# Recurrent gate products of 64 channels on the four quarters of the matmul array, second gate's tanh in two half-height pieces

## Chip, cores and metric

The kernel runs on one core of a Trainium2 chip. The time is the device time of one execution in microseconds (us). A core has a matmul engine (PE), a vector engine (DVE), an activation engine (ACT), GpSimd (POOL) and a sync engine (SP) that here only issues the loads of weights. Each has its own instruction stream, and they meet at semaphores.

## What is computed

One program computes two transformer-like layers, one after the other, for 512 tokens of width 1024. The change touches a small part of the first: the gates of a recurrent unit. There are 1024 channels in 16 blocks of 64, and each block has its own 64x64 weights for two gates:

```python
def rg_lru(x, wa, ba, wx, bx, lam):
    r = jax.nn.sigmoid(block_diag_linear(x, wa, ba).astype(jnp.float32))
    i = jax.nn.sigmoid(block_diag_linear(x, wx, bx).astype(jnp.float32))
    log_a = -LRU_C * r * jax.nn.softplus(-lam.astype(jnp.float32))
    a = jnp.exp(log_a)
    mult = jnp.sqrt(-jnp.expm1(2.0 * log_a))
    u = mult * (i * x.astype(jnp.float32))
    # then h[t] = a[t] * h[t-1] + u[t] along the tokens

# around it, for each token:
xc = causal_depthwise_conv(rnn_x, conv_w, conv_b)
y_rnn = rg_lru(xc, ...) * jax.nn.gelu(rnn_gate)
```

Before it, one projection (`h @ w_in`) gives all inputs of the layer, the recurrent ones among them; after it come sparse attention, the output projections and a feed-forward part, and then the second layer.

## The kernel before

Activations lie transposed: channels on the 128 partitions, the 512 tokens along the free dimension. Every large product is cut into "jobs" of 128 output channels. A job (`job`, `block_of`, lines 325 to 327) runs 24 matmuls of 128x512: for each of 8 slices of the contraction the products high*high, high*low and low*high of operands that were split into two parts. The weights of a job come by DMA (SP); ACT makes the high part (`split`, line 907), POOL subtracts it to get the low part in four pieces (line 296), and PE waits for `lo_ready`. Four weight slots are in flight. DVE takes each finished job out of PSUM (`take`, line 1450) and counts `job_taken`; a job waits until the one two before it was taken.

The jobs have one fixed order. The change lies in the recurrence, whose order is written out by hand in a loop of four turns (`for i in range(4)`, in each engine's stream). Each turn handles channel tiles f = 2i and 2i+1 of 128 channels (two blocks of 64 each):

- PE: job k+2, job k+3, `rnn_gates(2i)`, job k+4, `rnn_gates(2i+1)`, job k+5, with k = 15 + 4i. `rnn_gates` (line 433) waits for `conv_done` and issues two f32 matmuls of 128x512, one for each gate. Their weights `rgw` are a 128x128 matrix with two 64x64 blocks on the diagonal and zeros elsewhere. Each f32 matmul shows as two records.
- ACT: `gelu_square`, two `split`s, `conv_head(f+1)` (line 1009), `gelu_square`, then `rnn_decay(f)`, `gelu_tanh`, a `split`, `rnn_decay(f+1)`, `gelu_tanh`, a `split`, `conv_head(f+2)`, two square roots (`rnn_root`, line 1035) and two `rnn_high` (line 1039). `rnn_decay` (lines 1026 to 1031) is two tanh out of PSUM, a wait for their end, two exp and a third tanh.
- DVE: `take` of jobs k+2 and k+3, `conv_tail(f+1)`, two `gelu_inner`, `take` of k+4, `rnn_input(f)` and `rnn_input(f+1)` (each waits for `rnn_a`, the last instruction of `rnn_decay`), `take` of k+5, `conv_tail(f+2)`, `rnn_scan(f)` and `rnn_scan(f+1)` (wait for `rnn_root`; the scan is line 1593), and `rnn_low` of both, which wait for `rnn_high`.

In the fourth turn DVE has the maxima of the attention scores (line 1607) between `rnn_input(6)` and `rnn_input(7)`, and PE runs the first scores (line 440) after `rnn_gates(7)`. Then `pair(0)` begins: PE runs a job, turns the values (line 450) and waits for `rlo_ready` of 8, the low part of the recurrence's last tile, before the first job that multiplies the recurrence's output `b_hi`, `b_lo`. ACT's order in that place is `rnn_high(6)`, six exponentials (line 1073), a `split`, `rnn_high(7)`.

The two gates of a tile go to two PSUM banks: tiles alternate between `(s_ps[0], s_ps[1])` and `(s_ps[2], o_ps)`.

Of the kernel before, what the change touches and what calls it, by code (L numbers as in the profile page):

```python
# [29 lines left out]
ACT = mybir.ActivationFunctionType  # L30
# [3 lines left out]
P = 128  # L34
# [82 lines left out]
def build(nc, w_all, x_t, mem_t, vecs, consts, rg_w, consts2, row_table, out):  # L117
    with ExitStack() as ctx:
# [3 lines left out]
        def sem(name):  # L122
            return ctx.enter_context(nc.semaphore(name))
# [28 lines left out]
        def tiles(i, n=1):  # L152
            return arena[:, i:i + n, :]

        def flat(ap):
            return ap.rearrange("p a b -> p (a b)")
# [23 lines left out]
        rc = [arena[:, 2, :], arena[:, 3, :]]  # L180
        rr = [arena[:, 4, :], arena[:, 5, :]]
        ri = [arena[:, 6, :], arena[:, 7, :]]
        ra = [arena[:, 17, :], arena[:, 18, :]]
        rt = [arena[:, 8, :], arena[:, 19, :]]
        rgw = flat(tiles(24, 4)).rearrange("p (f c) -> p f c", c=2 * P)
# [44 lines left out]
        rnn_ps = ((s_ps[0], s_ps[1]), (s_ps[2], o_ps))  # L230
# [21 lines left out]
        def s(name):  # L252
            if name not in SEMS:
                SEMS[name] = sem(name)
            return SEMS[name]
# [59 lines left out]
        def _(pe):  # L315
            mm, tp = nc.tensor.matmul, nc.tensor.transpose

            def block_of(k, kts, hi, lo, n=T, last=7, pieces=False):

                sl, ps = k % SLOTS, bank(k)  # L320
                for kt in kts:
                    if pieces and kt % (KT // PIECES) == 0:
                        pe.wait_ge(s("lo_ready"), k * PIECES + kt * PIECES // KT + 1)
                    c = slice(kt * P, kt * P + P)
                    mm(ps[:, 0:n], w_hi[:, sl, c], hi[:, kt, 0:n], start=kt == 0, stop=False)  # L325
                    mm(ps[:, 0:n], w_hi[:, sl, c], lo[:, kt, 0:n], start=False, stop=False)  # L326
                    ins = mm(ps[:, 0:n], w_lo[:, sl, c], hi[:, kt, 0:n], start=False, stop=kt == last)  # L327
                return ins
# [59 lines left out]
            for t in range(QT):  # L388
                ins = tp(t_ps[1][:, t * P:t * P + P], p1[:, 0, t * P:t * P + P], ident)
# [22 lines left out]
            for k in range(8):  # L412
# [8 lines left out]
                for t in range(QT):  # L421
                    ins = mm(sums[:, t, 2 * k:2 * k + 2], sq[:, (k + 1) % 2, t * P:t * P + P], halves,
                             start=True, stop=True)
# [4 lines left out]
            def rnn_gates(f):  # L428

                u = f % 2  # L430
                pe.wait_ge(s("conv_done"), f + 1)
                for c in range(2):
                    ins = mm(rnn_ps[u][c][:], rgw[:, f, c * P:c * P + P], rc[u], start=True, stop=True)
                ins.then_inc(s("rnn_mm"), 1)

            def scores(p, which):
# [70 lines left out]
            for i in range(4):  # L507
                k = J_RNN + 4 * i
                job(k + 2, a_hi, a_lo)
                job(k + 3, a_hi, a_lo)  # L510
                rnn_gates(2 * i)
                job(k + 4, a_hi, a_lo)
                rnn_gates(2 * i + 1)
                if i == 3:
                    pe.wait_ge(s("k_normed"), 2)
                    pe.wait_ge(s("rnn_tanh"), 7)
                    scores(0, ATT_FIRST)
                job(k + 5, a_hi, a_lo)
# [42 lines left out]
            for c in range(2):  # L561
                ins = mm(s_ps[c][:], w_alpha[:, c * P:c * P + P], in2[:, 12, :], start=True, stop=True)
# [4 lines left out]
            for h in range(4):  # L567
# [4 lines left out]
                for t in range(QT):  # L572
                    ins = tp(t_ps[h % 2][:, t * P:t * P + P], in2[:, 4 + h, t * P:t * P + P], ident)
# [5 lines left out]
            for c in range(2):  # L579
                for t in range(QT):  # L580
                    ins = tp(t_ps[c][:, t * P:t * P + P], in2[:, 2 + c, t * P:t * P + P], ident)
# [17 lines left out]
            for m in range(4):  # L599
# [3 lines left out]
                for h in range(4):  # L603
                    out_r = slice(64 * (h % 2), 64 * (h % 2) + 64)
                    for n in (2 * m, 2 * m + 1)[0:1 if m == 3 else 2]:
                        r = slice(64 * (n % 2), 64 * (n % 2) + 64)
                        ins = mm(t_ps[n % 2][out_r, h * P:h * P + P], g_ke[r, m, h * 64:h * 64 + 64],
                                 g_vt[h][r, m, :], start=True, stop=True)
# [20 lines left out]
            for c2 in range(2):  # L629
# [7 lines left out]
                for half in range(2):  # L637
                    h = 2 * c2 + half
                    for t in range(QT):
                        c = slice(t * P, t * P + P)  # L640
                        mm((o_ps, s_ps[1])[half][:, c], g_vt[h][:, t, :], g_at[h][:, c], start=t == 0, stop=False,
                           skip_group_check=True)
                for n in range(1, 8):
                    for half in range(2):
                        r = slice(64 * half, 64 * half + 64)
                        c = slice(64 * n, 64 * n + 64)
                        ins = mm((o_ps, s_ps[1])[half][:, c], g_st[r, c2, n, :], g_qd[r, c2, c],
                                 start=False, stop=n == 7, skip_group_check=True)
# [9 lines left out]
            for t in range(QT):  # L658
                ins = tp(t_ps[0][:, t * P:t * P + P], in2[:, 18, t * P:t * P + P], ident)
# [200 lines left out]
            for gi, g in enumerate(FF2_GROUPS):  # L860
# [17 lines left out]
                for kt in (g - 2, g - 1):  # L878
                    pe.wait_ge(s("hlo_ready"), done - g + kt + 1)
                    ins = block_of(k, [kt], a_hi, a_lo, last=g - 1)  # L880
# [6 lines left out]
            for t in range(QT):  # L887
# [3 lines left out]
                ins = mm(sums[:, t, 20:22], sq[:, 1, t * P:t * P + P], ones2, start=False, stop=True)  # L891
# [6 lines left out]
        def _(act):  # L898
            fn = nc.scalar.activation
# [50 lines left out]
            for f in range(8):  # L950
# [16 lines left out]
               scale=float((64 ** -0.5) * (8 ** -0.5))).then_inc(s("iw_ready"), 1)  # L967
# [32 lines left out]
            def scol(c0, f):  # L1000
                return small[:, c0 + f:c0 + f + 1] if isinstance(f, int) else small[:, ds(f + c0, 1)]
# [18 lines left out]
            def rnn_decay(f):  # L1020

                u = f % 2
                act.wait_ge(s("rnn_mm"), f + 1)
                if f >= 2:
                    act.wait_ge(s("rlo_ready"), f - 1)
                fn(rr[u], rnn_ps[u][0][:], ACT.Tanh, scale=0.5, bias=scol(32, f)).then_inc(s("act_step"), 1)
                fn(ri[u], rnn_ps[u][1][:], ACT.Tanh, scale=0.5, bias=scol(40, f)).then_inc(s("rnn_tanh"), 1)
                act.wait_ge(s("rnn_tanh"), f + 1)
                fn(ra[u], rr[u], ACT.Exp, scale=scol(16, f), bias=scol(16, f)).then_inc(s("act_step"), 1)
                fn(rt[u], rr[u], ACT.Exp, scale=scol(8, f), bias=scol(8, f)).then_inc(s("act_step"), 1)  # L1030
                fn(rr[u], rr[u], ACT.Tanh, scale=scol(24, f), bias=scol(24, f)).then_inc(s("rnn_a"), 1)
# [10 lines left out]
            for i in range(4):  # L1042
                k, f = J_RNN + 4 * i, 2 * i
                gelu_square(f)
                split(k + 5)
                conv_head(f + 1)
                split(k + 6)
                gelu_square(f + 1)
                rnn_decay(f)
                gelu_tanh(f)  # L1050
                split(k + 7)
                rnn_decay(f + 1)
                gelu_tanh(f + 1)
                split(k + 8)
                if i < 3:
                    conv_head(f + 2)
                rnn_root(f)
                rnn_root(f + 1)
                if i < 3:
                    rnn_high(f)  # L1060
                    rnn_high(f + 1)
# [45 lines left out]
            with act.Fori(0, 2) as i:  # L1107
                for c in range(4):
# [4 lines left out]
                       bias=scol(56, i * 4 + c)).then_inc(s("sg_ready"), 1)  # L1113
# [1065 lines left out]
```

## Time and profile before

| | before |
|---|---|
| median of 3 runs | 1635.64 us (1634.28 to 1636.27) |
| the profiled execution | 1634.13 us, of it span 1632.3 us |
| PE busy | 1597.4 us (98%) |
| DVE busy | 722.0 us (44%) |
| ACT busy | 671.3 us (41%) |
| POOL busy | 797.6 us (49%) |

All times in the rows are counted from the span's start. A row of the timeline has start, length, engine, line, operation, output<-input, shape and count, and in brackets the idle time before it and who ended it. Matmul records overlap, so it is their starts that tell the pace. PEld are the weight loads. A row of the windows has, for a stretch, the busy time of PE, PEld, DVE, ACT and POOL, then the granted PE clock (1.00 is full), the share of the DMA engines and the rate.

### The profile page before, as it was taken

The numbers are of one execution on the slowest core, as the hardware profiler recorded it, in microseconds if no ns is written. First come the engines' busy times: TensorE is split into PE (matmuls) and PEld (weight loads), VectorE is DVE, ScalarE is ACT, GpSimd is POOL, SyncE is SP. The second block draws the span as 40 slices with busy tenths as digits, with TensorE's granted clock in tenths as the row PEclk, the third lists the DMA queues.
The fourth block names the chain that finished last, engine by engine and source line by source line (L and its number), as shares of the span: only waits on it lengthen the run. The fifth ranks groups of instructions, "written<-read, shape, count | busy, mean of one in ns | idle before, by whom it ended". The sixth has DMA issues, their size and how long they took to land. (4 is left out here: it accounts for less than half of the span.)

```text
span 1632.3 us, 22641 instructions
## 1 busy us (share of the span) xinstructions
PE 1597.4 (98%) x7646; PEld 1294.2 (79%) x7646; DVE 722.0 (44%) x1373; ACT 671.3 (41%) x1082; POOL 797.6 (49%) x1060
## 2 busy tenths in 40 slices
PE   7999998999999999999999999999999999999997
PEld 6787776777888888888888877678978888888886
DVE  5597996664233212121132442744223552452354
ACT  5415675544424423232233424643544442342332
POOL 5244573323454555555555541246635555565453
PEclk9999999999999999999999999999999999999999
DMA  5222221112323232323233222132422223223231
GB/s 185 87 84 78 72 92 64 52 65 104 103 90 103 91 103 90 103 90 103 90 101 103 90 79 65 41 113 94 129 77 91 91 90 116 90 90 104 90 103 65
DMA packets 45061, 149.77 MB, mean 92 GB/s; under 512 B 4600, under 2 KB 7808, under 8 KB 44992
## 3 DMA queue, kind: packets, MB, share of 16 engines
q1 hardware_dynamic: 38592, 139.48, 26.2%
q10 hardware_dynamic: 6400, 9.36, 1.7%
q8 instruction: 45, 0.74, 0.2%
q14 instruction: 24, 0.20, 0.0%
HBM read 146.58 MB, written 2.11 MB: 91 GB/s over the span
## 5 line engine op out<-in xcount | busy, mean ns | idle before, releaser
L296 POOL TENSOR_TENSOR w_lo<-w_raw,w_hi 128x256 fp32r<-128x256 f32 x1056 | 797.4, 787 | 810.6 <-ACT w_hi L907 809.8
L325 PE MATMUL job<-a_hi,w_hi 128*128 128x512 f32 (+1 forms) x1056 | 406.4, 385 | 10.0 <-POOL w_lo L296 9.8
L327 PE MATMUL job<-a_hi,w_lo 128*128 128x512 f32 (+1 forms) x1056 | 398.2, 377 | 0.0
L326 PE MATMUL job<-a_lo,w_hi 128*128 128x512 f32 (+1 forms) x1056 | 398.0, 377 | 0.0
L907 ACT ACTIVATE w_hi<-w_raw 128x1024 fp32r<-128x1024 f32 x264 | 275.1, 1050 | 281.2 <-PE job L327 271.5
L325 PE MATMUL job<-b_hi,w_hi 128*128 128x512 f32 x952 | 375.6, 395 | 5.1 <-DVE b_lo L1450 4.8
L327 PE MATMUL job<-b_hi,w_lo 128*128 128x512 f32 x952 | 371.3, 390 | 0.0
L326 PE MATMUL job<-b_lo,w_hi 128*128 128x512 f32 x952 | 371.0, 390 | 0.0
L325 PEld LDWEIGHTS job<-a_hi,w_hi 128*128 128x128 f32 x1056 | 199.0, 188 | 52.6 <-DVE a_lo L1447 11.0
L326 PEld LDWEIGHTS job<-a_lo,w_hi 128*128 128x128 f32 x1056 | 199.2, 189 | 37.2 <-issue 1.9
L327 PEld LDWEIGHTS job<-a_hi,w_lo 128*128 128x128 f32 x1056 | 199.0, 188 | 37.1
L325 PEld LDWEIGHTS job<-b_hi,w_hi 128*128 128x128 f32 x952 | 179.2, 188 | 42.5 <-DVE b_lo L1450 5.1
L327 PEld LDWEIGHTS job<-b_hi,w_lo 128*128 128x128 f32 x952 | 179.0, 188 | 37.8
L326 PEld LDWEIGHTS job<-b_lo,w_hi 128*128 128x128 f32 x952 | 179.2, 188 | 36.1 <-issue 0.2
L1450 DVE TENSOR_TENSOR arena<-arena,job 128x512 f32<-128x512 f32 (+1 forms) x92 | 62.9, 686 | 263.3 <-PE job L327 249.9
L1450 DVE TENSOR_TENSOR arena<-job,rstd 128x512 f32<-128x512 f32 (+1 forms) x117 | 80.0, 687 | 167.0 <-PE job L327 141.6
L1447 DVE SCALAR_TENSOR_TENSOR arena<-arena,vec 128x512 f32<-128x512 f32 x112 | 103.7, 926 | 60.4 <-ACT arena L1398 53.0
L922 ACT ACTIVATE sq<-arena 128x512 f32<-128x512 f32 x48 | 30.1, 630 | 114.8 <-DVE arena L1450 111.6
L1398 ACT ACTIVATE arena<-arena,vec 128x512 f32<-128x512 f32 x44 | 35.6, 809 | 87.8 <-DVE arena L1450 87.8
L1450 DVE TENSOR_TENSOR a_lo<-arena,a_hi 128x512 f32 (+1 forms) x58 | 40.0, 692 | 64.0 <-ACT a_hi L1129 42.2
L1128 ACT ACTIVATE arena<-arena 128x512 f32<-128x512 f32 x32 | 20.2, 632 | 106.5 <-DVE arena L1447 106.5
L1447 DVE SCALAR_TENSOR_TENSOR arena<-job,rstd 128x512 f32<-128x512 f32 x32 | 22.1, 691 | 91.2 <-PE job L327 86.6
(259 smaller groups left out, 1368.0 us busy)
## 6 DMA issues: line engine op xcount, KB each, us to landing
w_raw<-w_all SPq DMA_DIRECT2D x264, 512.0 KB, 3.4
arena<-x_t ACTq DMA_DIRECT2D x8, 512.0 KB, 6.9
arena<-rg_w ACTq DMA_DIRECT2D x1, 1024.0 KB, 7.8
arena<-row_table ACTq DMA_DIRECT2D x1, 1024.0 KB, 6.1
arena<-mem_t ACTq DMA_DIRECT2D x1, 1024.0 KB, 6.7
out_t<-arena SPq DMA_DIRECT2D x4, 256.0 KB, 2.2
out_t<-arena ACTq DMA_DIRECT2D x4, 256.0 KB, 2.2
arena<-consts ACTq DMA_DIRECT2D x1, 384.0 KB, 3.8
```

The costliest lines, as they stand in the source:

```text
L296: nc.gpsimd.tensor_tensor(w_lo[:, sl, c], raw[:, sl, c], w_hi[:, sl, c].bitcast(F32), ALU.subtract).then_inc(s("lo_ready"), 1)
L325: mm(ps[:, 0:n], w_hi[:, sl, c], hi[:, kt, 0:n], start=kt == 0, stop=False)
L326: mm(ps[:, 0:n], w_hi[:, sl, c], lo[:, kt, 0:n], start=False, stop=False)
L327: ins = mm(ps[:, 0:n], w_lo[:, sl, c], hi[:, kt, 0:n], start=False, stop=kt == last)
L907: fn(w_hi[:, sl], raw[:, sl], ACT.Copy).then_inc(s("hi_ready"), 1)
L922: fn(sq[:, f % 2, :], src, ACT.Square).then_inc(s("sq_ready"), 1)
L1128: fn(act_s[:, c % 2, :], act_t[:, c % 2, :], ACT.Square).then_inc(s("ff_sq"), 1)
L1398: fn(f_c[u], f_u[u][:, PAD:PAD + T], ACT.Identity, scale=vcol("conv_w2", col + 88), bias=vcol("conv_b2", col)).then_inc(s("f_head"), 1)
L1447: return v.scalar_tensor_tensor(out=out_, in0=a, scalar=sc, in1=b, op0=op0, op1=op1)
L1450: return v.tensor_tensor(out_, a, b, op)
```

## The change

`rnn_gates` issues four matmuls of 64 contraction rows and 64 output channels instead of two of 128 and 128; the zero blocks are no longer multiplied. The first gate's halves go to the same partitions as before. The second gate's halves are written to the other half of the partitions of their bank, so that the four products stand on four different quarters of the array. ACT puts them back: the second tanh becomes two instructions of 64 partitions and 512 columns, each reading one half of the bank and writing the other half of `ri`.

```diff
                 u = f % 2
                 pe.wait_ge(s("conv_done"), f + 1)
-                for c in range(2):
-                    ins = mm(rnn_ps[u][c][:], rgw[:, f, c * P:c * P + P], rc[u], start=True, stop=True)
+                for half in range(2):
+                    r, other = slice(64 * half, 64 * half + 64), slice(64 - 64 * half, P - 64 * half)
+                    mm(rnn_ps[u][0][r], rgw[r, f, 64 * half:64 * half + 64], rc[u][r], start=True, stop=True)
+                    ins = mm(rnn_ps[u][1][other], rgw[r, f, P + 64 * half:P + 64 * half + 64], rc[u][r],
+                             start=True, stop=True)
                 ins.then_inc(s("rnn_mm"), 1)
...
                 fn(rr[u], rnn_ps[u][0][:], ACT.Tanh, scale=0.5, bias=scol(32, f)).then_inc(s("act_step"), 1)
-                fn(ri[u], rnn_ps[u][1][:], ACT.Tanh, scale=0.5, bias=scol(40, f)).then_inc(s("rnn_tanh"), 1)
+                even, odd = slice(0, 64), slice(64, 128)
+                fn(ri[u][even], rnn_ps[u][1][odd], ACT.Tanh, scale=0.5, bias=scol(40, f)[even]).then_inc(s("act_step"), 1)
+                fn(ri[u][odd], rnn_ps[u][1][even], ACT.Tanh, scale=0.5, bias=scol(40, f)[odd]).then_inc(s("rnn_tanh"), 1)
                 act.wait_ge(s("rnn_tanh"), f + 1)
```

## Rows read from the trace of the kernel before

**Rows 1.** Windows of 10 us around the end of the recurrence.
```profile
235.00:245.00 10.00, 10.00 (x50) 7.63 (x47) 9.83 (x19) 7.36 (x10) 8.64 (x10) 1.00 0.38 114
245.00:255.00 10.00, 5.08 (x23) 3.53 (x21) 7.31 (x15) 8.00 (x21) 6.91 (x7) 0.85 0.26 96
```

**Rows 2.** Waits of PE from 100 to 262 us: total, times, longest.
```profile
PE job L325 <- DVE b_lo L1450: 4.8, 1, 4.8
```

**Rows 3.** Timeline of the gate products: weight loads of one set, starts of two sets.
```profile
149.11 0.19 PEld L433 LDWEIGHTS score<-arena 128*128 128x128 f32 x1 [0.24 <-issue]
149.54 0.19 PEld L433 LDWEIGHTS score<-arena 128*128 128x128 f32 x1 [0.24 <-issue]
...
173.97 1.88 PE L433 MATMUL score<-arena 128*128 128x512 f32 x4
...
224.56 1.88 PE L433 MATMUL score<-arena 128*128 128x512 f32 x4
```

**Rows 4.** Timeline of ACT over the third turn of the recurrence.
```profile
198.03 0.63 ACT L1039 ACTIVATE b_hi<-arena 128x512 fp32r<-128x512 f32 x1 [1.95 <-DVE arena L1447]
...
203.62 0.69 ACT L1026 ACTIVATE arena<-score,small 128x512 f32<-128x512 f32 x1
204.21 0.68 ACT L1027 ACTIVATE arena<-score,small 128x512 f32<-128x512 f32 x1
...
211.23 0.80 ACT L1031 ACTIVATE arena<-arena,small 128x512 f32<-128x512 f32 x1
...
223.46 0.63 ACT L1039 ACTIVATE b_hi<-arena 128x512 fp32r<-128x512 f32 x1 [1.96 <-DVE arena L1447]
```

**Rows 5.** Timeline of DVE over the same turn.
```profile
199.31 1.28 DVE L1450 TENSOR_TENSOR arena<-job,rstd 128x512 f32<-128x512 f32 x2
...
212.06 1.45 DVE L1447 SCALAR_TENSOR_TENSOR arena<-arena 128x512 f32<-128x512 f32 x2 [1.70 <-ACT arena L1031]
...
222.74 0.69 DVE L1447 SCALAR_TENSOR_TENSOR arena<-sq,arena 128x512 f32<-128x512 f32 x1
```

**Rows 6.** Timeline of ACT in the first turn and at the recurrence's end.
```profile
157.80 0.69 ACT L1026 ACTIVATE arena<-score,small 128x512 f32<-128x512 f32 x1 [1.26 <-PE o L433]
...
231.78 0.80 ACT L1031 ACTIVATE arena<-arena,small 128x512 f32<-128x512 f32 x1
...
240.24 1.15 ACT L1035 ACTIVATE arena<-arena 128x512 f32<-128x512 f32 x2
...
245.48 0.64 ACT L1039 ACTIVATE b_hi<-arena 128x512 fp32r<-128x512 f32 x1 [3.06 <-DVE arena L1447]
...
251.77 0.61 ACT L1039 ACTIVATE b_hi<-arena 128x512 fp32r<-128x512 f32 x1
```

**Rows 7.** Timeline of DVE at the recurrence's end.
```profile
232.14 0.68 DVE L1450 TENSOR_TENSOR arena<-job,rstd 128x512 f32<-128x512 f32 x1
...
238.57 1.83 DVE L1447 SCALAR_TENSOR_TENSOR arena<-arena 128x512 f32<-128x512 f32 x2
...
252.42 0.80 DVE L1450 TENSOR_TENSOR b_lo<-arena,b_hi 128x512 fp32r<-128x512 f32 x1 [2.42 <-ACT b_hi L1039]
```

**Rows 8.** Timeline of PE where the first job on the recurrence's output starts.
```profile
253.27 0.80 PE L325 MATMUL job<-b_hi,w_hi 128*128 128x512 f32 x1 [4.84 <-DVE b_lo L1450]
```

**Rows 9.** Timeline of PE in the second layer: 64x64 products, eight matmuls a row.
```profile
957.03 0.67 PE L607 MATMUL turn<-arena 64*64 64x128 f32 x16
963.30 0.67 PE L607 MATMUL turn<-arena 64*64 64x128 f32 x16
```

**Rows 10.** Timeline of PE in the second layer: a restart after idle time.
```profile
1023.24 0.71 PE L699 MATMUL turn<-cst,arena 128*128 128x128 f32 x3 [2.83 <-DVE arena L1454]
```

**Rows 11.** Windows behind the restarts of rows 8 and rows 10.
```profile
253.00:259.00 6.00, 4.67 (x15) 3.62 (x16) 5.58 (x22) 3.97 (x9) 2.42 (x3) 0.51 0.30 89
...
1024.00:1026.00 2.00, 2.00 (x6) 1.52 (x6) 1.93 (x8) 0.47 (x1) 0.50 (x1) 0.50 0.25 37
```

**Rows 12.** Groups of DVE by form: one operation on 64 partitions.
```profile
L1447 DVE SCALAR_TENSOR_TENSOR arena<-arena,vec,turn 64x512 f32<-64x512 f32 x1 | 0.7, 739 | 2.8 <-PE turn L366 2.8
```

## The prediction, as it was put on record

> **What bounds the kernel now.** I read the page first: PE is busy for 98% of the span, so the first guess is that every microsecond taken from PE is one gained. The question is whether that holds where the change is. The windows around the end of the recurrence show that it does not quite: from 235 to 245 us PE is busy throughout, and in the next 10 us it is busy for only 5.08, with a granted clock of 0.85 [rows 1]. The list of PE's waits names the cause: one wait of 4.8 us, for the low part of the recurrence's output [rows 2], which ends when PE restarts at 253.27 us [rows 8]. So the end of this stage is not set by PE. It is set by a chain through ACT and DVE, and the timelines of these two tell what that chain is made of.
>
> I followed it through the third turn of the loop. ACT's `rnn_high` at 198.03 us waits for DVE. From there ACT runs without a gap until its L1031 of the second tile, 211.23 + 0.80 = 212.03 us [rows 4]. DVE has been idle for 1.70 us by then and starts `rnn_input` on it at 212.06. From there DVE runs without a gap to the product that starts at 222.74 and ends at 223.43 us [rows 5], and ACT's next `rnn_high` starts at 223.46 [rows 4]. That is a closed ring of ACT and DVE with no PE in it, and one turn of it takes 223.46 - 198.03 = 25.43 us. PE's own turn is (224.56 - 173.97) / 2 = 25.30 us [rows 3]. PE is therefore level with the ring but no longer ahead of it. Only the first turn is different: there ACT waits 1.26 us for the gate products before it can start the tanh at 157.80 us [rows 6].
>
> **The change part by part.**
>
> *PE, removed and added.* The weight loads of a set are 0.43 us apart (149.54 - 149.11) [rows 3], there are four of them, so a set costs PE 1.72 us, and eight sets 13.8 us. The nearest rows to what replaces them are the 64x64 products of the second layer: eight matmuls of 128 columns, that is 16 records, take 0.67 us from first start to last end [rows 9]. A 128x512 record takes 0.43 us, so 16 records of 128 columns one after another would need 16 x 0.43 / 4 = 1.72 us; only if four quarters work at once do they fit. The path cost of that group is its repeat, 963.30 - 957.03 = 6.27 us, less the one job in it; four jobs and two gate sets make a turn of 25.30, so a job is (25.30 - 3.44) / 4 = 5.47 us, and the group costs 0.80 us against 0.43 of pure streaming. I charge the same 0.37 us on top of 2 x 0.43 for a new set: 1.23 us, a saving of about 0.5 us a set, 4 us in all, on PE. The bounds are 0.86 us a set (no charge) and 4 x 0.86 = 3.44 us (no overlap at all).
>
> The quarters of the new set differ from those rows in one thing: both halves of the rows write the same PSUM bank at the same time, on different partitions. Should that make them take turns, a set costs 1.72 us as before.
> The Trainium skill speaks on this against the change: the page "TensorEngine Tiling (Array Packing)", section "Restrictions and Gotchas", says that different row tiles cannot access the same PSUM bank simultaneously, by which a set would stay at 1.72 us; no row here shows two row halves in one bank.
>
> *ACT, added.* One more instruction in each `rnn_decay`. The step from the first tanh to the second is 204.21 - 203.62 = 0.59 us [rows 4]. The new pieces have half the partitions but all 512 columns. No ACT row has 64 partitions; a DVE operation on 64x512 took 0.739 us [rows 12], no less than its kin on 128 partitions (0.69 us in rows 5). So I take the full 0.59 us for each extra piece; the bounds are 0.3 (half, were it to go by partitions) and 0.7. Each turn has two of them, and both lie in ACT's part of the ring: +1.18 us a turn. What is queued behind the new instruction on ACT: the two exp, L1031, the gelu tanh, the `split` and all of the second `rnn_decay`. DVE waits for L1031, POOL for the `split` and PE through POOL; a job's low part is ready over 4 us before PE needs it, so the `split`s cost nothing as long as this margin is not used up.
>
> *The sum, on the path that sets the end.*
> - Turn 0: ACT no longer waits for PE. Its queue before the second tanh ends 1.26 us before 157.80, now 0.59 later: 157.13 us; PE's products are there by then (two sets faster by 0.5 each). So the second tile starts 0.67 earlier and has 0.59 more to do: -0.1 us. If PE stays at 1.72 a set, this is +0.6 instead.
> - Turns 1 and 2: the ring turns twice, from ACT's `rnn_high` of turn 0 to that of turn 2: 2 x 1.18 = +2.4 us. DVE's wait of 1.70 us for L1031 only moves: inside the turn the first L1031 comes 0.59 later and pushes DVE by some 0.4, which this wait takes in.
> - Turn 3: the second L1031 no longer decides, as DVE has the attention maxima before `rnn_input(7)`, which starts at 238.57 us [rows 7]. What counts is the first: L1031 ends at 231.78 + 0.80 = 232.58 us [rows 6], now 0.59 later, 233.17; DVE is through with its `take` at about 232.7 [rows 7]. DVE is pushed by 0.45 us. The square root at 240.24 us [rows 6] moves by 1.18 and comes just in time for the scan. From there the chain of `rnn_high(6)` at 245.48, the exponentials, `rnn_high(7)` at 251.77 [rows 6] and the low part at 252.42 us [rows 7] moves as one: +0.45 us.
> - Sum: -0.1 + 2.4 + 0.45 = +2.7 us for PE's restart at 253.27 us. After it PE is full again and all that follows moves along.
>
> PE's saving goes into its waits. In turns 1 to 3 job k+4 may not start before DVE has taken job k+2, at 199.31 + about 0.7 in the old timing [rows 5]; as the ring moves later and PE earlier, PE will stand still there for some 0.3 us in turn 1 and 2.5 us in turns 2 and 3, and the wait of 4.84 us [rows 8] grows to 6 or 7. Idle time has a price of its own: behind 2.83 us of it [rows 10] the granted clock was 0.50, the 1.2 GHz level, in a window of 2 us, and behind the wait of 4.84 us it was 0.51 over 6 us [rows 11]. A stretch of 2 to 6 us at the half level in turn 2 or 3 makes job k+4 end 1 to 3 us later; DVE's `take` of it and the next gate set have 1 to 2 us of room for that, so I count 0 here, with 0 to 1.4 us as bounds.
>
> The profiled execution took 1634.13 us; with 2.7 more it is 1636.8. It lies 1.5 us below the median of the runs shown, so against the median the forecast is 1635.64 + 2.7 = 1638.3 us.
>
> **The rivals.**
> 1. *The extra instructions lie on the ring (forecast).* 1638.3 us, by itself 1637.4 to 1639.5.
> 2. *The halves of one bank take turns.* PE gains nothing, ACT still pays: turn 0 gives +0.6 instead of -0.1, so 1639.0 us. PE's turn of 25.30 is still shorter than the ring's 26.6, so it costs no more than this. For it: no row has this pattern. Against it: the halves are on different partitions.
> 3. *Idle time brings the low clock into the loop.* Forecast or rival 2 plus up to 1.4 us, or a fall in more than one turn: 1639.5 to 1641.5 us. For it: the stop of 2.5 us is near the 2.83 us after which the clock was low. Against it: the next step that needs PE has 1 to 2 us of room.
> 4. *PE is the bound after all, and the change is faster.* If ACT's pieces cost 0.3 us each or if the ring had slack that I did not see, the ring would turn at PE's pace, and PE's 0.5 us a set would come through in the first three turns, 3 us, with the last turn still held by the tail: 1632.5 to 1635 us. It decides from the point where ACT's extra time per turn is below PE's saving and there is slack of over 1 us in the ring. Against it: ACT shows no gap between 198.03 and 212.03, DVE none from there to 223.43.
> 5. *The quarters do not overlap.* Then PE's turn is 25.30 + 2 x 1.72 = 28.7 us, PE is the bound, and the seven intervals to `rnn_gates(7)` plus that set cost about 8 x 1.72 = 13.8 us: about 1649 us. Rows 9 speak against it.
>
> **How the numbers follow.** The chances: forecast 0.54, rival 2 0.17, rival 3 0.19, rival 4 0.08, rival 5 0.02. The range reaches over the first three and the upper part of rival 4: 1635.5 to 1641.0 us. What a measurement of this kernel can tell from no change is about 0.2%, 3.3 us: 1632.4 to 1638.9. The forecast lies inside this, near its edge; of its own 0.54 I give 0.38 to "same" and 0.15 to "slower"; of rival 2 about half each; rival 3 is slower but for a small part; rival 4 is mostly "same". Together: faster 0.03, same 0.57, slower 0.40.
>
> **What would show it.** In the changed trace: a gate set with eight records whose starts lie within about 0.9 us and the next job about 1.2 us after the first; two tanh pieces of the second gate, of 0.68 us, 0.59 apart; ACT's `rnn_high` of turns 1 and 2 26.6 us apart instead of 25.43; new PE waits for DVE's `take` of about 2.5 us in turns 2 and 3; PE's restart on the recurrence's output at about 256 us after a wait of 6 to 7. Wrong would be: pieces of clearly less than 0.6 us, a ring that still turns in 25.4 us, a restart before 253.3 us, or a time that comes from anywhere behind the restart, where nothing of the change lies.

## The result, and the profile after

The changed kernel takes 1640.48 us (median of 11 runs, 1638.55 to 1640.80) against 1636.0 us for the kernel before in the same sessions (11 runs, 1634.28 to 1636.39): 4.5 us more, a ratio of 1.0026 with a 95% interval of 1.0018 to 1.0034. The forecast was 1638.3 us with a range of 1635.5 to 1641.0.

The page of the changed kernel, part 1: PE has as much work as before and a longer span.

```profile
span 1638.9 us, 22713 instructions
...
PE 1597.7 (97%) x7678; PEld 1293.1 (79%) x7678; DVE 716.6 (44%) x1373; ACT 677.6 (41%) x1090; POOL 793.9 (48%) x1060
```

The two profiled spans differ by 6.6 us, the medians by 4.5: the executions of either kernel fall into two groups about 1.7 us apart, and the profile of before is one of the lower group, that of after one of the upper. Part of the difference lies in the last 13 us, in code that the change does not touch: PE is busy there for 2.88 us at a clock of 0.66 before, and for 4.23 us at 0.53 after. The windows of the last 13 us, before first and after second:

```profile
1620.00:1633.00 13.00, 2.88 (x22) 2.61 (x22) 5.58 (x10) 2.18 (x3) 0.00 (x0) 0.66 0.43 162
```
```profile
1626.00:1639.00 13.00, 4.23 (x22) 3.84 (x22) 5.54 (x9) 1.35 (x2) 0.00 (x0) 0.53 0.43 162
```

So I compare the stretch in which the change acts: from ACT's first `conv_head` (145.76 us before, 146.17 after; the 0.41 is from the start of the program) to PE's restart on the recurrence's output. Before it ends at 253.27 us [rows 8], after at 257.98: 107.51 against 111.81 us, 4.30 more. That is nearly the whole of the 4.5.

**PE.** The timeline of PE in the changed kernel, one gate set and its neighbours:

```profile
209.36 0.39 PE L327 MATMUL job<-a_hi,w_lo 128*128 128x512 f32 x1
209.68 0.64 PE L434 MATMUL score<-arena 64*64 64x512 f32 x1
209.68 0.64 PE L435 MATMUL o<-arena 64*64 64x512 f32 x1
209.69 0.64 PE L434 MATMUL score<-arena 64*64 64x512 f32 x1
209.70 0.64 PE L435 MATMUL o<-arena 64*64 64x512 f32 x1
210.16 0.59 PE L434 MATMUL score<-arena 64*64 64x512 f32 x1
210.16 0.59 PE L435 MATMUL o<-arena 64*64 64x512 f32 x1
...
210.69 0.50 PE L325 MATMUL job<-a_hi,w_hi 128*128 128x512 f32 x1
211.03 0.39 PE L326 MATMUL job<-a_lo,w_hi 128*128 128x512 f32 x1
```

All four quarters start within 0.02 us, although the two of each gate write halves of one bank. From the record before the set to the second one of the next job it is 211.03 - 209.36 = 1.67 us; less two ordinary steps of 0.227, the set costs 1.22 us. The same two records around a set in the kernel before:

```profile
173.75 0.39 PE L327 MATMUL job<-a_hi,w_lo 128*128 128x512 f32 x1
...
175.92 0.40 PE L326 MATMUL job<-a_lo,w_hi 128*128 128x512 f32 x1
```

They are 2.17 us apart, less the same two steps 1.72 us, as [rows 3] say.

**Where PE's gain went.** PE's waits from 100 to 270 us in the changed kernel (before: only that of rows 2 is longer than 2 us):

```profile
PE job L325 <- DVE b_lo L1455: 6.5, 1, 6.5
PE job L325 <- DVE arena L1455: 4.6, 3, 2.7
PE turn L470 <- ACT acc L1071: 1.1, 1, 1.1
PE turn L453 <- DVE arena L1455: 0.4, 1, 0.4
```

The wait at the end has grown from 4.8 to 6.5 us, and there are three new ones (0.89, 2.65 and 1.02 us, one in each of the turns 1 to 3) for DVE's `take`. Behind the one of 2.65 us the clock was low for a while: PE's restart, and the windows around it, with 0.93 and 0.76 in the column of the clock.

```profile
202.40 0.47 PE L325 MATMUL job<-a_hi,w_hi 128*128 128x512 f32 x1 [2.65 <-DVE arena L1455]
```
```profile
200.00:204.00 4.00, 1.60 (x6) 1.36 (x7) 3.62 (x6) 3.70 (x6) 1.53 (x3) 0.93 0.00 0
204.00:210.00 6.00, 6.00 (x24) 4.45 (x26) 5.11 (x6) 5.88 (x9) 6.00 (x6) 0.76 0.29 87
```

**The ring.** ACT over the third turn, the lines that answer to [rows 4]:

```profile
200.30 0.63 ACT L1044 ACTIVATE b_hi<-arena 128x512 fp32r<-128x512 f32 x1 [1.96 <-DVE arena L1452]
...
205.89 0.69 ACT L1029 ACTIVATE arena<-score,small 128x512 f32<-128x512 f32 x1
206.60 0.69 ACT L1031 ACTIVATE arena<-score,small 64x512 f32<-64x512 f32 x1
207.31 0.68 ACT L1032 ACTIVATE arena<-score,small 64x512 f32<-64x512 f32 x1
208.03 0.81 ACT L1034 ACTIVATE arena<-arena,small 128x512 f32<-128x512 f32 x1
...
215.18 0.80 ACT L1036 ACTIVATE arena<-arena,small 128x512 f32<-128x512 f32 x1
...
227.26 0.63 ACT L1044 ACTIVATE b_hi<-arena 128x512 fp32r<-128x512 f32 x1 [1.95 <-DVE arena L1452]
```

A turn takes 227.26 - 200.30 = 26.96 us instead of 25.43 [rows 4], and ACT's part of it, from `rnn_high` to the end of the second L1036, 15.68 instead of 14.00: 0.84 for each of the two tanh groups. A piece of 64 partitions takes 0.69 us, as long as a full one; but the steps are 0.71 and 0.71 us, where the step between the two full tanh was 0.59. DVE's part is shorter by 0.16: its first two products after the second L1036 take 1.29 us together instead of 1.45 [rows 5], as POOL's burst now ends before they start. The 4.30 us of the stretch split as follows: turn 0, from the first `conv_head` to its second `rnn_high` at 173.32, +0.30; turns 1 and 2, 53.94 instead of 50.85, +3.09; turn 3 and the tail +0.91.

### The profile page after: what moved, and what is told of

Read it like the earlier page. It is cut to its first block and busy times, and to the rows that moved or that the text cites. A ratio compares the mean times of both kernels' runs of the same rounds, so it can differ in the third digit from the quotient of the medians.

```text
span 1638.9 us, 22713 instructions
## 1 busy us (share of the span) xinstructions
PE 1597.7 (97%) x7678; PEld 1293.1 (79%) x7678; DVE 716.6 (44%) x1373; ACT 677.6 (41%) x1090; POOL 793.9 (48%) x1060
```

## The experiments

Each kernel was timed beside the kernel before, in four sessions whose medians of before were 1636.00, 1635.96, 1636.04 and 1635.75 us; each ratio is taken inside its session. The stretch is that from the first `conv_head` to PE's restart, in the profiled execution; the last column is its difference to before.

| run | ratio to before (95%) | median us | stretch us | stretch against before |
|---|---|---|---|---|
| before | | 1636.0 | 107.51 | |
| the change | 1.0026 (1.0018 to 1.0034) | 1640.48 | 111.81 | +4.30 |
| quarters only | 0.9993 (0.9984 to 1.0002) | 1634.77 | 106.41 | -1.10 |
| halves only | 1.0029 (1.0018 to 1.0040) | 1640.65 | 111.75 | +4.24 |
| extra full tanh | 1.0016 (1.0007 to 1.0025) | 1638.27 | 110.47 | +2.96 |
| change, split moved | 1.0045 (1.0031 to 1.0058) | 1642.46 | 114.81 | +7.30 |
| change, early product | 1.0025 (1.0016 to 1.0034) | 1639.48 | 110.84 | +3.33 |
| before, early product | 0.9996 (0.9987 to 1.0005) | 1635.71 | 107.21 | -0.30 |
| before, `rnn_high(7)` early | 0.9987 (0.9978 to 0.9996) | 1633.19 | 105.04 | -2.47 |
| before, both | 0.9984 (0.9975 to 0.9993) | 1632.72 | 104.81 | -2.70 |
| both and copies early | 0.9969 (0.9958 to 0.9980) | 1630.20 | 104.79 | -2.72 |
| the same with the change | 0.9994 (0.9985 to 1.0003) | 1634.19 | 108.43 | +0.92 |
| the same with quarters only | 0.9962 (0.9948 to 0.9976) | 1629.42 | 103.51 | -4.00 |

**1. The quarters alone.** The changed kernel with the old second tanh, so that the second gate's halves stay swapped (it leaves out putting them back):

```diff
-                even, odd = slice(0, 64), slice(64, 128)
-                fn(ri[u][even], rnn_ps[u][1][odd], ...)
-                fn(ri[u][odd], rnn_ps[u][1][even], ...)
+                fn(ri[u], rnn_ps[u][1][:], ACT.Tanh, scale=0.5, bias=scol(40, f)).then_inc(s("rnn_tanh"), 1)
```

> Only the products change: four 64x64 quarters, and one full-height tanh of 128x512 for the second gate, so the two halves of that gate stay swapped (the part left out is the swap). Theory A (a ring of ACT and DVE sets the recurrence, PE does not): the ring keeps its 25.4 us a turn, only the first turn gains because ACT no longer waits 1.26 us for PE; PE's restart on the recurrence's output comes 0.7 to 1.0 us earlier than before, about 1635.2 us, ratio 0.9995. Theory B (PE is the bound and its saving of 0.5 us a set comes through): ring at PE's pace, 24.4 us a turn, restart 3 to 4 us earlier, about 1632.5 us, ratio 0.998.

1634.77 us, 1.2 less than before, of which the interval cannot tell the sign for certain; the stretch is 1.10 us shorter. The ring turns at its old pace, from 197.84 to 223.21 us in ACT's timeline, 25.37 us:

```profile
197.84 0.63 ACT L1042 ACTIVATE b_hi<-arena 128x512 fp32r<-128x512 f32 x1 [1.95 <-DVE arena L1450]
...
223.21 0.63 ACT L1042 ACTIVATE b_hi<-arena 128x512 fp32r<-128x512 f32 x1 [1.96 <-DVE arena L1450]
```

Eight sets at 0.5 us each would be 4 us; 1.1 arrive. The rest is in PE's waits: 6.2 us before the restart and 1.7 for `take`. That is theory A.

**2. The halves alone.** The kernel before with the second tanh in two straight pieces, each of which reads and writes the same half of the partitions (a crossed piece reads one half and writes the other):

```diff
-                fn(ri[u], rnn_ps[u][1][:], ACT.Tanh, scale=0.5, bias=scol(40, f)).then_inc(s("rnn_tanh"), 1)
+                even, odd = slice(0, 64), slice(64, 128)
+                fn(ri[u][even], rnn_ps[u][1][even], ACT.Tanh, scale=0.5, bias=scol(40, f)[even]).then_inc(s("act_step"), 1)
+                fn(ri[u][odd], rnn_ps[u][1][odd], ACT.Tanh, scale=0.5, bias=scol(40, f)[odd]).then_inc(s("rnn_tanh"), 1)
```

> Only the tanh changes: the old two 128x128 products, and the second tanh in two pieces of 64 partitions, each straight (no piece crosses to the other half). Theory A (the extra piece on the ring is the whole loss, and a piece of half height keeps the step from overlapping, 0.71 us instead of 0.59): rnn_decay 0.84 us longer, ring 26.9 to 27.0 us a turn, the first turn loses 0.85 more because it still waits for PE; restart about 4.8 us later than before, about 1641 us, ratio 1.003. Theory C (it is the crossing of halves that makes the steps 0.71 us, not the height): steps 0.59, rnn_decay 0.59 us longer, ring 26.4, restart about 3.3 us later, about 1639.3 us, ratio 1.002. Theory D (the loss comes from PE's new stops and the low clock, not from ACT): about the time before, ratio 1.000.

1640.65 us: without any quarter on PE the loss is as large. PE's stops for `take` sum up to 2.4 us here, and none has the low clock behind it (1.00 in both windows from 200 to 210 us), so theory D falls. That the total equals the changed kernel's is a coincidence of two differences. Its 4.24 us are 0.68 in turn 0, 2.80 in turns 1 and 2 and 0.76 behind them, where the changed kernel has 0.30, 3.09 and 0.91: turn 0 still waits for the old products, and each group is cheaper. ACT's timeline gives the steps:

```profile
205.72 0.69 ACT L1026 ACTIVATE arena<-score,small 128x512 f32<-128x512 f32 x1
206.31 0.67 ACT L1028 ACTIVATE arena<-score,small 64x512 f32<-64x512 f32 x1
207.01 0.69 ACT L1029 ACTIVATE arena<-score,small 64x512 f32<-64x512 f32 x1
207.73 0.82 ACT L1031 ACTIVATE arena<-arena,small 128x512 f32<-128x512 f32 x1
```

Neither of my two readings of the step holds as written. From the full tanh to the even half the step is 0.59, from the even to the odd half 0.70. So it is not the height, and it is not only the crossing.

**3. One more full tanh.** The kernel before with

```diff
+                fn(rt[u], rnn_ps[u][1][:], ACT.Tanh, scale=0.5, bias=scol(40, f)).then_inc(s("act_step"), 1)
                 fn(ri[u], rnn_ps[u][1][:], ACT.Tanh, scale=0.5, bias=scol(40, f)).then_inc(s("rnn_tanh"), 1)
```

> The old products and the old second tanh, with one extra full-height tanh of 128x512 of the same PSUM bank ahead of it, written to a tile that is free then. It measures what one more ACT instruction costs with all three at full height. If the height is what makes the steps 0.71 us: steps 0.59, rnn_decay 0.59 us longer, ring 26.4 us, about 1639.3 us, ratio 1.002. If any third tanh costs 0.85 us: the same as the halves-only run, ring 27.0 us, about 1641 us.

```profile
205.10 0.69 ACT L1026 ACTIVATE arena<-score,small 128x512 f32<-128x512 f32 x1
205.69 0.68 ACT L1027 ACTIVATE arena<-score,small 128x512 f32<-128x512 f32 x1
206.26 0.69 ACT L1028 ACTIVATE arena<-score,small 128x512 f32<-128x512 f32 x1
206.98 0.81 ACT L1030 ACTIVATE arena<-arena,small 128x512 f32<-128x512 f32 x1
```

Steps of 0.59 and 0.57 us: one more instruction of full height costs the 0.58 that I had put into the forecast, and the ring turns in 26.43 us (199.51 to 225.94). The time is 1638.27, what the forecast had for the changed kernel, 1638.3. With the runs 2 and 3 and the changed kernel beside each other, the steps are 0.56 to 0.59 us where source and target start at the same partition as those of the instruction ahead, and 0.68 to 0.72 us in every step where they do not. The cleanest pair is full to straight (0.59) against full to crossed (0.71): height, target and bias are the same, and only the source starts at partition 64 instead of 0. In the other long steps source and target change together, and one piece of 64 partitions follows another, so a change of the target alone, and two half pieces with the same start, stay untested. The changed kernel has two long steps in each group (full to crossed, crossed to crossed), the straight halves have one, the full tanh none: `rnn_decay` is longer by 0.84, 0.72 and 0.58 us.

**4. A split moved on ACT.** The changed kernel with

```diff
                 rnn_decay(f)
                 gelu_tanh(f)
-                split(k + 7)
                 rnn_decay(f + 1)
+                split(k + 7)
                 gelu_tanh(f + 1)
```

> The changed kernel with one weight split (0.95 us of ACT) moved from between the two rnn_decay of a turn to behind the second. It touches nothing on PE or in the gates. Theory A (ring): ACT's part of the ring is 0.95 us shorter, of which the gelu tanh takes back some 0.2; ring about 26.2 us a turn instead of 26.97; the square roots of the last turn keep their place behind the same instructions, so restart 1.5 to 2.3 us earlier than in the changed kernel, about 1638.5 us, ratio to before 1.0015. Theory D (PE's stops are the cause, ACT is not the bound): no change against the changed kernel, 1640.5 us, ratio 1.0027.

1642.46 us: 2 us slower than the changed kernel, where I had expected 2 us faster; a miss. A turn takes 230.12 - 202.09 = 28.03 us. ACT's part is shorter as expected (202.09 to 216.98, 14.89 instead of 15.68 us), but DVE's part, from the start on L1036 to the end of its last product, has grown from 11.21 to 13.07 us. In the timelines of DVE and POOL:

```profile
223.52 1.22 DVE L1455 TENSOR_TENSOR arena<-arena 128x512 f32<-128x512 f32 x1
224.78 1.64 DVE L1598 TENSOR_TENSOR_SCAN arena<-arena 128x512 f32<-128x512 f32 x1
226.45 1.04 DVE L1452 SCALAR_TENSOR_TENSOR arena<-sq,arena 128x512 f32<-128x512 f32 x1
```
```profile
218.00 8.94 POOL L296 TENSOR_TENSOR w_lo<-w_raw,w_hi 128x256 fp32r<-128x256 f32 x8 [5.89 <-ACT w_hi L910]
```

and in the changed kernel:

```profile
217.53 3.97 POOL L296 TENSOR_TENSOR w_lo<-w_raw,w_hi 128x256 fp32r<-128x256 f32 x4 [2.49 <-ACT w_hi L910]
```
```profile
221.97 0.68 DVE L1455 TENSOR_TENSOR arena<-arena 128x512 f32<-128x512 f32 x1
222.69 1.23 DVE L1598 TENSOR_TENSOR_SCAN arena<-arena 128x512 f32<-128x512 f32 x1
```

The two splits now lie side by side, POOL works on both in one burst of 8.9 us, and under it the same DVE operations take 1.22 instead of 0.68 and 1.64 instead of 1.23 us. DVE also waits 0.17 us for the gelu tanh, which now comes behind a split. The time still follows the ring; what failed was my claim that the move touches nothing else on it. That the operations take longer while POOL works is what these durations show; what the two engines contend for was not tested.

**5 and 6. The product that does not need all of `rnn_decay`.** In DVE's `rnn_input`, in the changed kernel (5) and in the kernel before (6):

```diff
-                dve.wait_ge(s("rnn_a"), f + 1)
+                dve.wait_ge(s("rnn_tanh"), f + 1)
                 dve.wait_ge(s("conv_done"), f + 1)
                 did(stt(ri[u], ri[u], 1.0, rc[u], ALU.add, ALU.mult))
+                dve.wait_ge(s("rnn_a"), f + 1)
                 stt(rt[u], rt[u], 1.0, rr[u], ALU.add, ALU.mult).then_inc(s("rnn_m"), 1)
```

> The changed kernel; DVE's first product of rnn_input (the one that uses the second gate) waits for the two tanh pieces instead of the last instruction of rnn_decay, so 0.61 us of DVE leave the ring and nothing on ACT, PE or POOL changes. Theory A (ring of ACT and DVE): ring 26.97 - 0.6 = 26.4 us a turn, three turns of it: PE's restart 1.8 us earlier than in the changed kernel, stretch from the first conv_head to the restart 110.0 us against 111.8; about 1638.7 us, ratio to before 1.0017. Theory D (PE's stops are the cause): no change, 1640.5 us.

> The kernel before with the same move. Theory A: the ring could turn in 24.8 us, but PE's turn is 25.3, so PE becomes the bound of turns 1 and 2: 25.3 us a turn, restart 0.4 to 1.0 us earlier than before, about 1635.2 us, ratio 0.9995. If the ring had been bound by PE already: no change, 1636.0 us.

5: 1639.48 us, a ratio of 1.0025 that cannot be told from the changed kernel's 1.0026. The stretch can: it is 0.97 us shorter with PE untouched, and the ring takes 26.72 us, 0.25 less and not the 0.6 that I expected, so half of the expected gain came. The timeline of DVE shows who is next, `conv_head` on ACT:

```profile
217.61 3.62 DVE L1452 SCALAR_TENSOR_TENSOR arena<-arena,vec 128x512 f32<-128x512 f32 x3 [0.16 <-ACT arena L1012]
```

So the ring has a second path of nearly the same length, over ACT alone up to `conv_head(f+2)`, and both hold the two pieces. 6: 1635.71 us, 0.3 less, too little to tell from before. Turn 1 still takes 25.42 us and turn 2 25.29, 0.14 less. In turn 2 DVE now waits 0.22 us for PE's job in the middle of the ring, where it had no such wait: ring and PE meet at 25.3 us, as in the expectation, but its range of 0.4 to 1.0 us was too high.

```profile
214.18 0.69 DVE L1450 TENSOR_TENSOR arena<-job,rstd 128x512 f32<-128x512 f32 x1 [0.22 <-PE job L327]
```

**7 and 8. The tail.** The kernel before with `rnn_high(7)` ahead of three exponentials and a split (7), and with the early product too (8):

```diff
-                exponentials(p, ATT_FIRST)
+                exponentials(p, ATT_FIRST[:3])
+                if p == 0:
+                    rnn_high(7)
+                exponentials(p, ATT_FIRST[3:])
                 split(J_MIX + 2 * p + 4)
-                if p == 0:
-                    rnn_high(7)
```

> The kernel before with ACT's rnn_high(7) after three of the six exponentials instead of after all six and a split. It touches only the tail between the recurrence and PE's restart. If the restart hangs on this instruction, it comes 2.3 us earlier (DVE has the recurrence's last output at 249.4 us, ACT converts it 2.3 us later); the wait of PE falls from 4.8 to 2.5 us, and if the low clock behind it stays out or is shorter, up to 2.6 us more: 1631 to 1634 us, ratio 0.997 to 0.999. If the tail is bound by something else: 1636 us.

> The kernel before with both moves. If the two act on different parts of the same chain, the gains add: restart 2.7 to 3.3 us earlier than before, 1630.5 to 1633.5 us, ratio 0.997 to 0.9985. If PE is the bound by then, no more than the tail's move alone.

7: 1633.19 us, 8: 1632.72 us. In 7 the restart is 2.47 us earlier, as the tail's rows said [rows 6, 7], but behind it PE now waits 2.57 us for ACT's copies, and the clock is 0.50 in the window behind that (before: 0.51 [rows 11]). 8 has the restart 2.70 us earlier, the two gains added (2.47 and 0.30); its median is 0.5 us below that of 7, which the intervals do not tell apart. PE in 7:

```profile
250.81 0.50 PE L325 MATMUL job<-b_hi,w_hi 128*128 128x512 f32 x1 [2.38 <-DVE b_lo L1451]
...
254.35 1.97 PE L467 MATMUL turn<-cst,arena 128*128 128x128 f32 x8 [2.57 <-ACT acc L1066]
```
```profile
254.00:259.00 5.00, 4.65 (x16) 3.97 (x17) 3.22 (x13) 2.10 (x4) 1.51 (x3) 0.50 0.36 108
```

**9, 10, 11. The change where the tail is short.** 9 is 8 with ACT's copies (`values`) ahead of the split; 10 is 9 with the whole change; 11 is 9 with the quarters and one full tanh, and leaves out putting the halves back.

```diff
                 exponentials(p, ATT_FIRST[3:])
+                if p == 0:
+                    values()
                 split(J_MIX + 2 * p + 4)
                 exponentials(p, ATT_LAST)
-                if p == 0:
-                    values()
```

> The kernel before with both moves of the last run, and ACT's copies of the turned values (line 1066) ahead of the split and the last two exponentials. In the run with both moves PE waits 2.56 us more for these copies, right behind its restart. If ACT's order sets that wait, it goes down to what the turned probabilities need, 0 to 1.5 us: 1631 to 1632.5 us, ratio 0.997 to 0.9985. If the probabilities of DVE end last there: 1632.7 us as before this move.

> The last kernel with the whole change on top: four quarters and two crossed pieces. Theory A (ring of ACT and DVE): the ring is set by the pieces again, about 26.7 us a turn, and the change costs about what it cost before: 3.5 to 4.5 us over the kernel without it, 1635 to 1637 us. Rival (the change would have paid if the tail had been short, because PE's saving was hidden by the wait before the restart): 1 to 4 us below the kernel without it.

> The last kernel with the four quarters and one full-height tanh (the second gate's halves stay swapped: the swap is left out). It bounds what the quarters could give if the swap cost nothing. With the early product PE's turn of 25.3 us is as long as the ring's, so here the saving of 0.5 us a set can come through until the ring is met again, near 25.1 us a turn: 0.5 to 2 us below the kernel without it, 1629.5 to 1631.5 us.

9 takes 1630.20 us, 5.6 less than the 1635.75 us of before in the same session (0.9969, 0.9958 to 0.9980), and the fastest of those that leave nothing out. It lies below the 1631 to 1632.5 us that I expected. Its stretch is no shorter than that of 8; the gain lies behind the restart, where the second wait is 0.75 us instead of 2.56, and now ends on DVE:

```profile
252.36 1.68 PE L467 MATMUL turn<-cst,arena 128*128 128x128 f32 x8 [0.75 <-DVE arena L1455]
```

10 takes 1634.19 us: on a kernel 5.6 us faster the change costs 4.0 us more, and its stretch is longer by 108.43 - 104.79 = 3.64 us. So it was not the long wait in the tail that hid a gain. 11 takes 1629.42 us, 0.8 less than 9, which the intervals (0.9962 and 0.9969 to before) do not tell apart; its stretch is 1.28 us shorter and its turns 1 and 2 take 25.23 and 25.19 us instead of 25.42 and 25.28. By the stretches, the quarters without the price of the swap are worth 1.1 to 1.3 us, here and in run 1.

## Why the prediction was right, and where its size was off

*The bound.* Right: the ring of ACT and DVE, read from the two timelines, sets the recurrence. The quarters alone bring 1.1 of 4 us, two half-height pieces alone bring a loss as large as the change's, and one more full tanh, with nothing changed on PE, brings 2.96 us.

*PE's part.* Right to 0.01 us: 1.23 us a set were predicted from the 64x64 group of the second layer, 1.22 were measured. Rival 5 falls with it, and rival 2 too: the four quarters of a set start within 0.02 us, on different partitions of the banks. The rule of the Trainium skill ("TensorEngine Tiling (Array Packing)", "Restrictions and Gotchas") by which row halves in one bank cannot go together is not borne out for this pattern.

*ACT's part.* This term was mis-sized: 0.59 us for an extra piece, measured 0.84. I took the step between two full tanh and asked only whether half height makes it shorter. That it could be longer stood as a bound of 0.7, and even that was too low for a group, because I priced only the added step: the step from the first tanh to the second gate's first piece grew too, from 0.59 to 0.71. Two steps of 0.71 in place of one of 0.59 are 0.83, with the roundings the 0.84. The full-height experiment shows that the 0.58 of the forecast was right for an instruction that starts where the last one did.

*Turn by turn.* Turn 0: -0.1 predicted, +0.30 measured; the sum was -1.26 + 2 x 0.59, and with 0.84 it is +0.42; the rest is that without a wait the tanh starts 0.1 us before the split ahead of it ends, so the wait was worth 1.35. Turns 1 and 2: +2.4 predicted, +3.09 measured; 4 x 0.84 are 3.36, less 0.11 and 0.16 from DVE, of which less overlaps POOL's bursts. Turn 3: +0.45 predicted by way of the first L1031, +0.91 measured. Here the step named the wrong predecessor: DVE waited 0.86 us for the second L1036 and then 1.52 us for the square root, which the prediction had coming "just in time"; two groups of 0.84 instead of 0.59 put it 0.5 us later than predicted, and behind DVE. The 1.52 us are longer than this 0.5 because DVE was also early: its products in front of this place, which had POOL's burst beside them before (1.83 us for two [rows 7]), took 1.29 us. The product that waits for the square root started 18.19 us after the turn's start on ACT at 223.46 (241.65, the first line below), now 19.14 us after it at 227.26 (246.40): 0.95 us later, which is the 0.91. DVE before, then ACT and DVE in the changed kernel:

```profile
241.65 1.05 DVE L1450 TENSOR_TENSOR arena<-arena 128x512 f32<-128x512 f32 x1
```
```profile
245.73 1.16 ACT L1040 ACTIVATE arena<-arena 128x512 f32<-128x512 f32 x2
```
```profile
242.98 1.29 DVE L1452 SCALAR_TENSOR_TENSOR arena<-arena 128x512 f32<-128x512 f32 x2 [0.86 <-ACT arena L1036]
...
246.40 1.01 DVE L1455 TENSOR_TENSOR arena<-arena 128x512 f32<-128x512 f32 x1 [1.52 <-ACT arena L1040]
```

*PE's stops and the clock.* Predicted: 0.3, 2.5 and 2.5 us; measured 0.89, 2.65 and 1.02. The third is shorter by about what the low clock behind the second (rival 3) took: the job of turn 2 lasts from 202.40 to the set at 209.68, 7.3 us instead of 5.5. DVE waited 0.82 us for that job, but then stood still for another 3.67 us until the second L1036, so it had room. So the low clock came, and cost nothing on the ring: turn 2, with a clock of 0.76 in it, takes 26.96 us, and turn 1, with 1.00, takes 26.98.

*The chances.* The measured +4.5 us lies inside the stated range and beyond the 0.2% that I called the limit of "same", on the side that had 0.40 against 0.57. By the number alone rival 3 would have won: 1640.48 us lies above the 1637.4 to 1639.5 that the forecast had for itself and inside rival 3's 1639.5 to 1641.5, and its low clock did come. The two turns above show that this is a coincidence: the 2 us between forecast and result are ACT's step. With 0.84 in the place of 0.59 the same sum gives 0.42 + 4 x 0.84 + (0.45 + 0.25) = +4.5 us. That this meets the median so well is partly luck, since turn by turn it is 0.1 and 0.3 too high and 0.2 too low.

## What to carry to other kernels

Before crediting a saving on the engine that is 98% busy, follow the chain through the other engines over one turn of the loop and compare the two periods: here 25.43 against 25.30 us, and what was added to the ring was paid nearly in full (3.09 of 3.36 us in two turns), while 0.5 us a set on PE bought about 1 us of 4. A layout that helps the matmul but needs a swap is paid per instruction where it is undone: 64 partitions took ACT as long as 128 (0.69 us). The gain was where the profile's one long wait ended: three moves of a few lines gave 5.6 us, nearly all of it from the two in the order of ACT's instructions, as DVE's early product alone could not be told from nothing.

## What the runs showed of the hardware

- ACT, back to back, 512 columns: the step to the next activation was 0.56 to 0.59 us when source and target start at the same partition as those of the one ahead (also from 128 partitions to the lower 64), and 0.68 to 0.72 when the source alone or both start at another one; each instruction takes 0.66 to 0.69 us either way. Only tanh out of PSUM was measured, and the target alone was not.
- Four 64x64 f32 products of 512 columns on the four quarters start within 0.02 us, with two row halves in each of two banks on different partitions, and the set costs 1.22 us on PE's path, 0.36 over the 0.86 of its columns.
- The same DVE product took 0.68 us alone and 1.22 us while POOL worked on a burst, the scan 1.23 and 1.64 us.
